# Order of work at the changes of stage in a two-model forward pass: low parts on GpSimd in half slots, the second half of x ahead of slots 2 and 3

## The reference, cut to what matters

```python
for i in range(4):      # first model
    out = (ssd_mixer, fox_mixer, mla_mixer, s5_mixer)[i](h, ...)   # h @ w_in ... @ w_out
    h = layer_norm(ALPHA * h + out, ln_g[i], ln_b[i])
...
x = x + mixed @ w_out                                   # second model, one layer
x = x + memory_cross_attention(rms_norm_2(x, g_cross), rms_norm_2(mem, g_mem), ...)
x = x + conv_glu_ffn(rms_norm_2(x, g_ffn), ...)
return rms_norm_2(x, g_final)
```

## Time and profile before

| | |
|---|---|
| median of three runs | 3759.97 us |
| the profiled execution | 3761.13 us |
| its span | 3759.1 us |
| TensorE, VectorE, ScalarE, GpSimd busy | 92%, 65%, 42%, 6% |
| mean granted clock of TensorE | 0.967 of 2.4 GHz |
| DMA, mean over the span | 171 GB/s |
| transfer of one slot (raw from the stream) | 4.8 us to landing |

### The profile page before, as it was taken

The page is one execution under the profiler, slowest core; times in us unless marked ns, Lnnn a source line. Parts: engine busy times, 40 slices in busy tenths (PEclk is TensorE's granted clock), DMA queues, the critical chain, the costliest instruction groups (busy, mean ns, idle before and its releaser), DMA issues.

```text
span 3759.1 us, 48741 instructions
## 1 busy us (share of the span) xinstructions
PE 3441.3 (92%) x18186; PEld 2942.3 (78%) x18186; DVE 2433.9 (65%) x3129; ACT 1567.1 (42%) x1857; POOL 227.6 (6%) x241
## 2 busy tenths in 40 slices
PE   6899999979999998888799999888998899999998
PEld 5777787767888877777799888778887688888886
DVE  4677777775555565555799966756556565655655
ACT  3344444434444343333467654333333344344342
POOL 0000000010000013000323200100001100000000
PEclk8899999989999999999999999999999899999999
DMA  5455555535444543333323245665665355555553
GB/s 211 146 196 195 190 190 190 190 130 197 177 175 179 177 165 135 120 126 123 120 106 103 101 158 201 189 227 210 228 233 191 123 198 184 186 191 179 190 188 124
DMA packets 89265, 642.83 MB, mean 171 GB/s; under 512 B 10177, under 2 KB 10257, under 8 KB 11713
## 3 DMA queue, kind: packets, MB, share of 16 engines
q1 hardware_dynamic: 83376, 607.16, 45.0%
q0 software_dynamic: 5776, 34.13, 2.8%
HBM read 638.02 MB, written 3.23 MB: 171 GB/s over the span
## 4 chain that ended last, share of the span: by engine, by line
PE 55%; DVE 17%; issue 16%; DVEq 5%; ACT 3%; DMA 3%; POOL 1%; ACTq 0%; POOLq 0%; SPq 0%
PE banks L705 15%; PE banks L706 15%; PE banks L707 15%; DVE WL L679 6%; DMA raw<-in_stream 2%; ACT WH L671 2%; DVE xc L1288 1%; DVEq L2477 1%; PE banks L761 1%; PE banks L762 1%; PE banks L763 1%; PE banks L722 1%; PE banks L1014 1%; PE banks L723 1%; PE banks L724 1%
## 5 line engine op out<-in xcount | busy, mean ns | idle before, releaser
L679 DVE TENSOR_TENSOR WL<-raw,WH 128x2048 fp32r<-128x2048 f32 (+2 forms) x565 | 1226.8, 2174 | 678.2 <-ACT WH L671 669.7
L671 ACT ACTIVATE WH<-raw 128x2048 fp32r<-128x2048 f32 (+2 forms) x575 | 1045.5, 1821 | 1075.9 <-DMA raw<-in_stream 547.1
L705 PE MATMUL banks<-WH,XH 128*128 128x512 f32 (+2 forms) x2784 | 1071.4, 385 | 86.5 <-DVE WL L679 41.2
L707 PE MATMUL banks<-WH,XL 128*128 128x512 f32 (+2 forms) x2784 | 1045.4, 375 | 0.0
L706 PE MATMUL banks<-WL,XH 128*128 128x512 f32 (+2 forms) x2784 | 1045.3, 375 | 0.0
L705 PEld LDWEIGHTS banks<-WH,XH 128*128 128x128 f32 x2784 | 536.0, 193 | 185.7 <-issue 76.6
L707 PEld LDWEIGHTS banks<-WH,XL 128*128 128x128 f32 x2784 | 535.8, 192 | 82.5
L706 PEld LDWEIGHTS banks<-WL,XH 128*128 128x128 f32 x2784 | 537.3, 193 | 77.6 <-issue 0.5
L705 PE MATMUL banks<-WH,YH 128*128 128x512 f32 x976 | 395.2, 405 | 13.6 <-DVE acc L802 8.5
L706 PE MATMUL banks<-WL,YH 128*128 128x512 f32 x976 | 389.0, 399 | 0.0
L707 PE MATMUL banks<-WH,YL 128*128 128x512 f32 x976 | 387.5, 397 | 0.0
(11 more groups left out here) (412 smaller groups left out, 3578.9 us busy)
## 6 DMA issues: line engine op xcount, KB each, us to landing
raw<-in_stream SPq DMA_DIRECT2D x575, 1024.0 KB, 4.8
gain<-in_gains POOLq DMA_DIRECT2D x9, 1024.0 KB, 5.1
arow<-acs_scratch POOLq DMA_DIRECT2D x8, 1024.0 KB, 4.9
offs<-in_ln_b POOLq DMA_DIRECT2D x4, 1024.0 KB, 8.2
acc<-in_x SPq DMA_DIRECT2D x2, 1024.0 KB, 6.7
src<-in_mem POOLq DMA_DIRECT2D x1, 2048.0 KB, 8.5
toep<-rvec_scratch POOLq DMA_DIRECT2D x4, 512.0 KB, 8.6
out_y<-src SPq DMA_DIRECT2D x2, 1024.0 KB, 3.9
```

The lines of the kernel that those rows point to most:

```text
L671: nc.scalar.activation(WH[:, n.first % PARTS, at], raw[:, n.first % RAWS, at], ACT.Copy).then_inc(hi_ready, 1)
L679: nc.vector.tensor_tensor(WL[:, n.first % PARTS, at], raw[:, n.first % RAWS, at], WH[:, n.first % PARTS, at].bitcast(F32), ALU.subtract).t ...
L705: nc.tensor.matmul(out, xh[:, k0 + k, at], wh[:, k, lo:hi], start=start, stop=False)
L707: ins = nc.tensor.matmul(out, xl[:, k0 + k, at], wh[:, k, lo:hi], start=False, stop=stop)
```

## The change

```diff
@@ first_lows (GpSimd)
-            at = slice(0, slot_width(At(n)))
-            nc.gpsimd.tensor_tensor(WL[:, n % PARTS, at], raw[:, n % RAWS, at], WH[:, n % PARTS, at].bitcast(F32),
-                                    ALU.subtract).then_inc(lo_ready, 1)
+            half = slot_width(At(n)) // 2
+            for lo in (0, half):
+                at = slice(lo, lo + half)
+                ins = nc.gpsimd.tensor_tensor(WL[:, n % PARTS, at], raw[:, n % RAWS, at],
+                                              WH[:, n % PARTS, at].bitcast(F32), ALU.subtract)
+            ins.then_inc(lo_ready, 1)
@@ first_products (TensorE)
-        for s in range(3):
+        for s in range(2):
             pe.wait_ge(xl_ready, 8 * i + s + 1)
             products(pe, n.plus(s), 4, width, pair, s == 0, False, k0=4 * s, tts=(0,), done=False)
         turn_groups(pe, i, source, 4, 6)
-        for s in range(3):
+        for s in range(2):
             pe.wait_ge(xl_ready, 8 * i + 4 + s + 1)
             products(pe, n.plus(s), 4, width, pair, s == 0, False, k0=4 * s, tts=(1,))
-            if s < 2:
-                turn_groups(pe, i, source, 6 + s, 7 + s)
+            turn_groups(pe, i, source, 6 + s, 7 + s)
+        pe.wait_ge(xl_ready, 8 * i + 7)
+        products(pe, n.plus(2), 4, width, pair, False, False, k0=8)
         pe.wait_ge(xl_ready, 8 * i + 8)
         products(pe, n.plus(3), 4, width, pair, False, True, k0=12)
@@ last_out (VectorE)
-        add_half(dve, slot, 1, 0)
+        for c in range(3):
+            add_half(dve, slot, 1, c)
         if i is not None:
             turn_low(dve, i, 0, 2)
-        add_half(dve, slot, 1, 1)
-        if i is not None:
-            turn_low(dve, i, 2, 4)
-        add_half(dve, slot, 1, 2)
         add_half(dve, slot, 1, 3)
         norm(dve, 1)
         if i is not None:
+            turn_low(dve, i, 2, 6)
             dve.wait_ge(lo_ready, slot + 3 + LEAD)
             split_low(dve, At(slot + 3 + LEAD))
-            turn_low(dve, i, 4, 6)
+            turn_low(dve, i, 6, 7)
             split_low(dve, At(slot + 4 + LEAD), True)
-            turn_low(dve, i, 6, 8)
+            turn_low(dve, i, 7, 8)
@@ last_splits (ScalarE)
         split_high(act, At(slot + 3 + LEAD))
         if i is not None:
+            turn_high(act, i, 4, 6)
             split_high(act, At(slot + 4 + LEAD), True)
-            turn_high(act, i, 4, 8)
+            turn_high(act, i, 6, 8)
```

## The result

The changed kernel takes 3733.09 us (median of four runs, 3727.65 to 3737.45) against 3758.31 before (3756.48 to 3760.03): ratio 0.9932, 95% interval 0.9915 to 0.9949, or 25.2 us less. On a second chip it took 3732.29 against 3760.5, ratio 0.9928 (0.9912 to 0.9944). The forecast was 3738 with a range of 3728 to 3752. The profiled execution took 3730.8 us, its span is 3728.8.

The account below looks back on a forecast made before the run. TensorE was 92% busy, so only its waits counted, the largest 41.2 us for VectorE's low parts. Terms of 24.2 us less 2 for the clock left 22: 3761.1 to 3739, 3738 in the median's terms, range 3728 to 3752.

Parts of the forecast that it names:

- The mechanism and the five changes: Stage starts: second half's first block moves earlier, gaining fox 4.4, mla 3.1, s5 0, cross 5.2, ffn 5.3 us.
- The alternation on SBUF: VectorE's norm and GpSimd's half slots take turns; in mla slot 1's low part 1.5 us late, norm's end 1.0.
- two other ways: In mla, slot 1's low part at 1351.0 if VectorE keeps its pair together, 1348.5 if GpSimd keeps its halves together.
- Groups 2 and 3 behind the norm: VectorE no longer does these groups of x before the norm, a pair taking 1.29 us; no instruction added or removed.
- S5: Start of s5, whose products wait for group 4 at once: 0.3 us, ends −1.0 and +1.0, taken as 0.
- Fox's restart: No term for fox; in cross an earlier slot 6 split before ScalarE's result copy gave 2.5 us, ends 0 and 3.3.
- The clock: 2 us taken off: TensorE, new gaps before slot 1 in fox and mla: half clock at about 2 in 3, costing 2 us together.
- ssd: Ssd's start, only first_products changed: turning x before slot 2 gains 3.7 us, ends 0 and 4.3.
- It does nothing: Rival, 7%: raw stream decides, slot 4 is released late and the gain is waited for at slot 4 or 5; 3760.
- Half: Rival, 22%: clock falls in new gaps of four changes (8 us), ssd's start gives nothing; gain 10 us, 3750.
- Slower: Rival, 4%: two gaps keep TensorE at 1.2 GHz over more blocks, 34 us lost against 24 gained; 3770.
- More: Rival, 12%: GpSimd keeps the boundary, no slow block, mix gives 2 us; gain 29 us, 3731.

Follow-up runs that it names:

- Early4: The kernel before with slot 4's split moved ahead of x's group 7 on ScalarE and VectorE, in fox and cross only: 3754.52 us, ratio 0.9979.
- ssd_old: The changed kernel with the old order of first products at ssd's start only: 3736.68 us, ratio 0.9934 to the kernel before.
- half_only: The kernel before with GpSimd's low parts in half slots and nothing else: ratio 0.9991 (0.9980 to 1.0002).

## Why the prediction was right, and where not

*The mechanism and the five changes.* Right. The second half's first block was placed by adding up the instructions ahead of group 4: forecast gains of 4.4, 3.1, 5.2 and 5.3 us stand beside 4.4, 3.6, 4.2 and 5.5. The second profile of the changed kernel has 4.4, 3.0 and 5.0 for fox, mla and cross. But in two of the four the agreement is partly luck. In fox the prediction called most of its 4.4 us the slow block in front of the turning. That block ran slow after the change too (4.41 us for 4.40, one slot earlier); the norm ended 14.6 us from GpSimd's start where 15.1 were forecast, and the two errors cancelled. In cross the 5.2 us counted on a stretch at half clock that the same order doesn't have in every profile; against the two that lack it the gain is 1.4 to 2.4 us.

*The alternation on SBUF.* Right in kind and nearly in size. I had taken alternate turns over two other ways; the rows of 1.31, 3.33 and 3.37 us show them, and mla and s5 have the same 3.33 and 3.37 us. What followed from it was a little too long. In mla, counted from GpSimd's start, slot 1's low part is ready at 10.58 us and not 10.82, the second norm piece ends 1.09 us behind it and not 1.25, and the norm's last two pieces begin at 12.11 and not 12.57. So the norm ends 0.4 us late and not 1.0. GpSimd's four halves took 10.58 us; 9.6 for the instructions and 1.0 for the wait, forecast 9.74 and 1.2. The price of the second instruction of a slot is 0.19 us (twice 2.394 less 4.60), where I had taken 0.2.

*Half slots.* The prediction gave them no gain of their own, and the runs give none: 0.9991 on the kernel before; 0.9928 against 0.9926 in the changed one. If they do anything by themselves, it is too small for these runs.

*Groups 2 and 3 behind the norm.* I had counted this as moved work. It looks like a small loss (0.9910 for 0.9928, with intervals that overlap): while GpSimd has the port, VectorE can still do what reads one operand in a bank, and this is such work. Put behind the norm, it stands in front of group 4.

*S5: the failed term was small.* Forecast 0.3, taken as 0; it is 1.0. The forecast had 1.1 us for the later norm and 1.2 for groups 2 and 3, against 2.28 for slot 2's low part; with VectorE's wait of 0.37 us for ScalarE at group 4, which stood there before, that is 0.3. The norm is only 0.45 us later, as in mla, and with that the same sum gives 1.0.

*Fox's restart: a term of the sum mis-sized, 2.5 us for 0.* For cross I had followed ScalarE's copy behind slot 6's split and found 2.5 us; the wait where the queries are turned fell from 4.64 us to 2.35, and 2.51 in the second profile. For fox I had not looked beyond the first products, though the same queue stands there: slot 4's low part came at 861.22, behind group 7 and the scaling, so slot 6 landed at 868.5, and slot 7's split and the gates stood behind it. Early4 shows that the restart by itself turns the gates with 2.5 us less waiting, and the changed kernel waits 2.5 and 2.3 us less there in its two profiles. From start to start fox gained 8.3 us in the first profile, 4.4 of it locally, but 6.8 in the second and in ssd_old, which has the same order in fox. The difference of 1.5 us between the two profiles of one kernel goes with the clock, and is not the restart: in the first profile it was 0.90 in 850 to 885 us, in the second 0.85, the same as in 860 to 895 of the kernel before.

*The clock: 2 us taken off.* Right in kind, and a matter of chance from place to place. The gap before slot 1 was followed by half clock in fox: the block from 833.76 to the turning at 838.17 took 4.41 us, in both profiles of the changed kernel. In mla, behind 2.84 us, it took 2.85; in the second profile, behind 2.83 us at the same place, 4.36 (granted 0.61). In cross, where the prediction had none, it took 4.41 us behind 1.87. A slow block cost 1.5 us, where the prediction allowed up to 2.85.

```profile
833.76 0.47 PE L708 MATMUL banks<-WH,XH 128*128 128x512 f32 x1 [2.14 <-POOL WL L691]
838.17 1.04 PE L848 MATMUL banks<-con,acc 128*128 128x128 f32 x8
```

The same kernel's second profile, slot 1 into mla:

```profile
1337.22 0.77 PE L708 MATMUL banks<-WH,XH 128*128 128x512 f32 x1 [2.83 <-POOL WL L691]
```

*The sum.* 22 us forecast, 25.2 and 28 measured in the two series. By the first pair of profiles the terms of ssd 4.1, of the changes 18.7, and of the restarts 2.5 and 2.3 make 27.6. With ssd at 2.9 (from the means of twelve profiles; 3.7 were forecast) and cross at some 1.9 (against the profiles without the slow block) they make about 24. Of the measured gains 25.2 lies between these two and 28 just above them. The single profiles scatter more: between 1406 and 1760 us of the trace before, where nothing was changed, the lead grows by 3 us in one profile of the changed kernel and by 5.4 in the other, and half_only gains 2.1 there too. That is why the difference of one pair of profiles (30.3) is not taken as the result.

*The rivals.* "It does nothing" is refuted, and no wait has come up at slots 4 and 5. "Half" would have needed half clock in every gap; before slot 1 it came in fox and cross in the first profile, in fox and mla in the second, and in ffn in neither. "Slower" is refuted. "More" (3731) stands nearer to the measured 3733 than the forecast does, but not for its reasons: GpSimd did not keep the boundary (VectorE's first norm instruction came between its third and fourth half), and a slow block did come in fox; what the forecast lacks for certain is fox's restart. Of the signs of being wrong, the second half's first block moved ahead by 7.2, 6.5, 7.0 and 8.4 us in fox, mla, cross and ffn; in the second profile mla has 5.8, just under the 6 that I had set, because of the slow block.

## What to carry to other kernels

At a change of stage, write down for each engine what stands ahead of the first piece that the next stage can't do without, and move behind it all that only later pieces need; here that was worth 3.0 to 5.5 us at three of the changes, 1.0 in s5, and 1.4 to 5.0 in cross, where the clock of the profile decides. Look at the granted clock of both profiles before a local difference is booked as a gain. Then follow the transfer queue past the place you changed: a split that is late by its position holds back the transfer two places on, and what stands behind that one on the same engine. Work on operands in a bank is what to give VectorE while GpSimd reads SBUF; and see whether what is won there is still there at the next wait (in fox it was not).

## What the runs showed of the hardware

- VectorE with two inputs in SBUF and GpSimd take turns by whole instructions, also when both have the next one ready: 3.33 us for GpSimd's 2.39, 3.37 for VectorE's 1.24. The Trainium skill, page SBUF — State Buffer, section SBUF: two separate sides, has the lock for the whole instruction, and these rows agree; that back-to-back instructions alternate is from the rows alone.
- Instructions with one operand in a bank did not wait: x's groups kept 1.27 us a pair during GpSimd's low parts (1331.07 in mla), as outside them (1.28 and 1.29).
- Splitting a 128x2048 subtraction on GpSimd in two costs 0.19 us.
- The length of one gap alone did not decide the clock of TensorE. Behind 2.84 us of idleness at slot 1 into mla the block ran at full clock (2.85 us), and behind 2.83 us at the same place of the same kernel at half clock (4.36 us, granted 0.61). Behind 3.07 and 3.06 us at slot 2 of cross in the old order it took 5.26 us (granted 0.50) and 2.82 us (1.00). Gaps of 1.87 and 2.14 us were followed by half clock too (4.41 us each, cross and fox).
